# A hybrid diffusion-transformer block on one Trainium2 core: the softmax shift of the grouped-query attention in one step, its bound as the exponentials' bias, and one tile in ten cast by GpSimd

## The reference, cut to what matters

```python
q_l = apply_rope(rms_norm(q_l, qk_g_q[l]), cos, sin)
k_l = apply_rope(rms_norm(k_l, qk_g_k[l]), cos, sin)
k_c = rms_norm(k_c, qk_g_k[l])
gqa_l = gqa_latent(q_l, concatenate([k_c, k_l]), concatenate([v_c, v_l]))

s = jnp.einsum('bqkgd,bskd->bkgqs', qg, k).astype(jnp.float32) * ATTN_SCALE
p = jax.nn.softmax(s, axis=-1).astype(v.dtype)
o = jnp.einsum('bkgqs,bskd->bqkgd', p, v)
```

## Time and profile before

| | us |
|---|---|
| runs | 1312.24, 1308.78, 1311.92 |
| median | 1311.92 |
| the profiled execution | 1312.07 |
| its span, first to last instruction | 1310.3 |
| TensorE busy in it | 1261.5 |
| VectorE busy | 941.1 |
| ScalarE busy | 660.0 |
| GpSimd busy | 295.4 |

### The profile page before, as it was taken

One profiled execution on the slowest core, in us unless ns is written; L12 is line 12 of the kernel. 1 busy time (PEld: TensorE's weight loads), 2 busy tenths in 40 slices (PEclk: granted clock), 3 DMA queues, 4 the chain that ended last, 5 costly groups with the idle time before them and its releaser, 6 DMA issues. The chain is left out here.

```text
span 1310.3 us, 22666 instructions
## 1 busy us (share of the span) xinstructions
PE 1261.5 (96%) x7808; PEld 655.4 (50%) x7808; DVE 941.1 (72%) x1577; ACT 660.0 (50%) x1256; POOL 295.4 (23%) x285
## 2 busy tenths in 40 slices
PE   7999999999898999999999999999999999999997
PEld 1564656444674566665455444444444444444443
DVE  3879887576688999983356976666666666566387
ACT  2532124444697999993225554444445444312225
POOL 0100000121133678851002233333322220000001
PEclk9999999999999999999999999999999999999999
DMA  9637712051330131011112122222322204997953
GB/s 374 231 106 284 285 33 65 1 162 65 103 142 1 34 128 32 0 33 49 49 49 81 50 85 71 77 80 80 88 88 88 80 24 146 312 341 257 361 186 131
DMA packets 106708, 158.89 MB, mean 121 GB/s; under 512 B 8208, under 2 KB 67088, under 8 KB 104848
## 3 DMA queue, kind: packets, MB, share of 16 engines
q1 hardware_dynamic: 106640, 158.00, 35.2%
HBM read 135.95 MB, written 19.93 MB: 119 GB/s over the span
## 5 line engine op out<-in xcount | busy, mean ns | idle before, releaser
L1100 PE MATMUL PS<-arena 128*128 128x512 f16 (+9 forms) x7208 | 1212.6, 328 | 29.4 <-DVE arena L2622 9.2
L1100 PEld LDWEIGHTS PS<-arena 128*128 128x128 f16 (+3 forms) x7208 | 604.0, 102 | 608.7 <-issue 60.4
L2702 DVE SCALAR_TENSOR_TENSOR arena<-arena 128x512 f16<-128x512 f32 x148 | 120.9, 823 | 75.6 <-ACT arena L2004 75.6
L2004 ACT ACTIVATE arena<-arena 128x512 f16<-128x512 f32 x140 | 87.6, 629 | 130.4 <-PE PS L1100 130.4
L2116 ACT ACTIVATE arena<-arena 128x512 f16<-128x512 f32 x77 | 48.2, 629 | 130.3 <-DVE arena L2850 72.7
L2607 DVE TENSOR_REDUCE arena<-PS 128x1 f32<-128x512 f32 (+1 forms) x160 | 103.5, 673 | 2.6 <-PE PS L1100 2.5
L1940 ACT ACTIVATE arena<-PS 128x512 f16<-128x512 f32 x160 | 101.4, 634 | 3.1 <-PE PS L1100 2.5
L1015 POOL TENSOR_TENSOR arena<-arena 128x512 f16<-128x512 f32 x64 | 73.9, 1155 | 55.1 <-ACT arena L1943 55.1
L980 POOL TENSOR_TENSOR arena<-arena 128x2 f32<-128x2 f32 (+1 forms) x18 | 21.1, 1172 | 262.1 <-DVE arena L2461 262.1
L1067 POOL TENSOR_TENSOR arena<-arena 128x512 f32<-128x512 f32 x20 | 26.3, 1319 | 221.6 <-DMA arena<-in_w_ffn_in 182.9
L2865 DVE SCALAR_TENSOR_TENSOR arena<-arena 128x512 f16<-128x512 f32 x77 | 52.1, 686 | 28.2 <-ACT arena L2116 28.2
(11 more groups left out here) (199 smaller groups left out, 1120.9 us busy)
## 6 DMA issues: line engine op xcount, KB each, us to landing
arena<-in_w_ffn_out SPq DMA_DIRECT2D x121, 256.0 KB, 5.5
arena<-in_w_mod SPq DMA_DIRECT2D x24, 1024.0 KB, 7.2
arena<-in_w_ffn_in SPq DMA_DIRECT2D x88, 256.0 KB, 3.0
arena<-in_w_in SPq DMA_DIRECT2D x9, 1024.0 KB, 5.4
left_operands<-arena SPq DMA_DIRECT2D x33, 256.0 KB, 2.2
arena<-left_operands SPq DMA_DIRECT2D x3, 2816.0 KB, 14.0
arena<-lay_bias SPq DMA_DIRECT2D x4, 1536.0 KB, 9.6
arena<-in_x SPq DMA_DIRECT2D x2, 2048.0 KB, 13.1
```

What stands on the lines that cost most here:

```text
L1100: return pe.matmul(out, lhsT, rhs, start=start, stop=stop, skip_group_check=True)
L2004: act.activation(aS[n % RING][:, 0], weight_block(p, b), ACT.Copy, scale=WS).then_inc(blk_hi, 1)
L2702: dve.scalar_tensor_tensor(dst[:, 1], src, WS, dst[:, 0], ALU.mult, ALU.subtract).then_inc(blk_lo, 1)
```

## The change

The shift is now one fp16 row: the negated maximum goes straight, rounded to fp16, from the reduction into `shifts`; the row of `lo` stays zero. The same rounded number shifts all scores of a query, so the softmax isn't changed by the rounding. The bound `shift1` isn't added to it any more; it stands as bias (a column of 128x1 in SBUF) in both exponentials, and its factor grows from 1 to 1.125. `mx` is doubled, for the two key heads. Of tile 4 (`CAST_TILE`) ScalarE takes only the fp32 exponential, and GpSimd casts it to fp16 ahead of its subtraction. `pt_hi` isn't counted in this stage any more.

```diff
-POOL_TILES = (1, 4, 6, 8)
+POOL_TILES, CAST_TILE = (1, 4, 6, 8), 4
...
-        mx, nm, rg = f32(3.0, GROUP, 3), f32(3.0625, GROUP), f32(3.09375, 2, GROUP)
+        mx, rg = f32(3.0, 2, GROUP, 3), f32(3.09375, 2, GROUP)
...
                 pool.wait_ge(s_exp, NNA + n + 1)
                 pt = Pt[n % RING_P]
+                if s.i == CAST_TILE:
+                    if n >= RING_P:
+                        pool.wait_ge(o_mm, NNA + n - RING_P + 1)
+                    own.step(pool.tensor_copy(pt[:, 0], Pf[s.full]))
+                    own.wait()
                 pool.tensor_tensor(pt[:, 1], Pf[s.full], pt[:, 0], ALU.subtract).then_inc(pt_lo2, 1)
...
             def turn_shifts(s):
-                pe.wait_ge(sh_rdy, 3 * s.g + 3)
+                pe.wait_ge(sh_rdy, s.g + 1)
...
                 act.wait_ge(st_mm, s.n + 1)
-                if s.s >= RING_P:
-                    act.wait_ge(o_mm, NNA + s.n - RING_P + 1)
-                act.activation(Pt[s.s % RING_P][:, 0], PS[:, s.bank], ACT.Exp).then_inc(pt_hi, 1)
+                if s.i != CAST_TILE:
+                    if s.s >= RING_P:
+                        act.wait_ge(o_mm, NNA + s.n - RING_P + 1)
+                    act.activation(Pt[s.s % RING_P][:, 0], PS[:, s.bank], ACT.Exp, bias=shift1)
                 if s.by_pool and s.s >= NKT:
                     act.wait_ge(pt_lo2, s.ahead(-NKT).n_low())
-                act.activation(Pf[s.full] if s.by_pool else PS[:, s.bank], PS[:, s.bank], ACT.Exp).then_inc(s_exp, 1)
+                act.activation(Pf[s.full] if s.by_pool else PS[:, s.bank], PS[:, s.bank], ACT.Exp, bias=shift1)\
+                    .then_inc(s_exp, 1)
...
                 dve.wait_ge(s_mm, NNA + c.n + 1)
+                if c.i == 0 and c.s >= 2 * NKT:
+                    dve.wait_ge(sh_rdy, c.g - 1)
...
             def query_shifts(c):
 
-                hi, lo = shifts[:, HD:HD + 3 * (P + 1) + 1:P + 1], shifts[:, HD + GROUP:HD + GROUP + 3 * (P + 1) + 1:P + 1]
                 dve.wait_ge(s_max, NNA + c.n + 1)
-                dve.tensor_reduce(nm, mx, AX, ALU.max, negate=True).then_inc(sh_rdy, 1)
-                dve.wait_ge(sh_rdy, 3 * c.g + 1)
-                dve.wait_ge(q2_hi, 1)
-                if c.s >= NKT:
+                if c.s < NKT:
+                    dve.wait_ge(q2_hi, 1)
+                else:
                     dve.wait_ge(sh_mm, c.g)
-                dve.tensor_tensor(hi, nm, shift1.broadcast_to((P, GROUP)), ALU.add).then_inc(sh_rdy, 1)
-                dve.wait_ge(sh_rdy, 3 * c.g + 2)
-                dve.scalar_tensor_tensor(lo, nm, shift1, hi, ALU.add, ALU.subtract).then_inc(sh_rdy, 1)
+                dve.tensor_reduce(shifts[:, HD:HD + (GROUP - 1) * (P + 1) + 1:P + 1], mx[:, c.kv], AX, ALU.max, negate=True)\
+                    .then_inc(sh_rdy, 1)
...
-            own.step(dve.tensor_scalar(shift1, shift1, -2.0 ** -7, math.log(PSC), ALU.mult, ALU.add))
+            own.step(dve.tensor_scalar(shift1, shift1, -1.125 * 2.0 ** -7, math.log(PSC), ALU.mult, ALU.add))
```

More of the change, by code:

```diff
@@ L539, in build @@
         s_max = sem("score_maximum")
-        sh_rdy = sem("shift_steps")
+        sh_rdy = sem("shift_ready")
         sh_mm = sem("shift_transposed")
@@ L2600, in chunk_maximum @@
                 dve.wait_ge(s_mm, NNA + c.n + 1)
+                if c.i == 0 and c.s >= 2 * NKT:
+                    dve.wait_ge(sh_rdy, c.g - 1)
                 ps = PS[:, CHUNK_BANK[c.s % 2]]
                 if c.i < 2 * GROUP:
-                    out = mx[:, c.i // 2, c.i % 2:c.i % 2 + 1]
+                    out = mx[:, c.kv, c.i // 2, c.i % 2:c.i % 2 + 1]
                 else:
                     h = 2 * (c.i - 2 * GROUP)
-                    out, ps = mx[:, h:h + 2, 2], ps.rearrange("p (h k) -> p h k", h=2)
+                    out, ps = mx[:, c.kv, h:h + 2, 2], ps.rearrange("p (h k) -> p h k", h=2)
                 dve.tensor_reduce(out, ps, AX, ALU.max).then_inc(s_max, 1)
```

## The result

The kernel after takes 1325.2 us (median of 4 runs, 1323.54 to 1326.57), the kernel before 1312.08 (4 runs, 1308.78 to 1313.31): a ratio of 1.0103, with a 95% interval of 1.0082 to 1.0125. It is slower by 13.1 us, where 17.5 were forecast. A second series of the same two gave 1325.27 us and a ratio of 1.0093 (1.0075 to 1.0111). The profiled execution took 1325.33 us, with a span of 1323.5, 13.2 more than before.

The account below looks back on a forecast made before the run. ScalarE was taken to pace the grouped-query stage; its group, 11.07 - 0.475 + 19 x 0.093 = 12.36 us, gave -0.5, +2.3, +14.2 and +1.5, together +17.5 us on 1312.1: 1329.6 us, range 1318 to 1336.

Parts of the forecast that it names:

- The bound of the kernel now: Grouped-query stage: ScalarE alone, gapless, makes a group last 11.07 us; VectorE is full in the four groups before 461 us.
- middle groups: Eleven full groups of the grouped-query stage, each 12.36 us in place of 11.07: +14.2 us.
- the entry: Start of the grouped-query stage: TensorE can start the shifts at about 412.97 in place of 413.44, giving -0.5 us.
- the copy of the outputs: ScalarE's 128-partition read of PSUM in each group, given the 0.47 us left of 11.07 after 10.60.
- The shift in one step: VectorE's three small instructions, 1.32 us, become one reduction of 0.2 us; its group falls to about 9.95; 0.47 us gained at entry.
- The cast: Tile 4: ScalarE saves one exponential, 0.475 us a group, 7.6 us in all; GpSimd's group goes from 9.32 to about 10.0.
- The column: Bound as 128x1 SBUF bias: 0.093 us for each of 19 exponentials a group, bounds nothing and 0.11.
- groups 1 to 3: Three groups to 461.39 us take 37.1 us in place of 34.8: +2.3 us.
- the last group and what is behind: Tile 9 before the last copy of shifts and the whole last group: +0.19 + 1.29 = +1.5 us.
- The free bias: Rival: each exponential's bias column costs 0 in place of 0.093 us; a group of 10.6 us, 1301.9 us in all; chance 0.08.
- GpSimd as the bound: Rival: GpSimd paces the groups, for which it would need 12.4 us a group; about 1331 us; chance 0.01.
- The clock's case: Rival: TensorE, idling 1.8 us or more a group, is sometimes granted its lower clock (1.2 GHz); 1330 to 1338 us; chance 0.05.

Follow-up runs that it names:

- e_row_nocast: e_row with CAST_TILE set to None, so ScalarE takes both exponentials of tile 4 again, leaving the one-step shift alone: 1307.3 us, ratio 0.9964 to the kernel before.
- e_cast_only: The kernel before with only the cast of tile 4 moved to GpSimd: 1306.6 us, ratio 0.9960 to the kernel before.
- e_row: The kernel after with the bound written once into the zero row of shifts, no bias column in either exponential: 1301.8 us, ratio 0.9921 to the kernel before.
- e_imm: The kernel after with the number -2.0 as bias of both exponentials, no column, the bound left out: 1303.0 us, ratio 0.9942 to the kernel before.
- e_nocast: The kernel after with CAST_TILE set to None, both exponentials of tile 4 on ScalarE with their column: 1337.3 us, ratio 1.0190 to the kernel before.

## Why the prediction was right, and where it was off

*The bound of the kernel now.* ScalarE paces the middle groups, VectorE the first four: e_row_nocast shows both (middle groups unchanged, the first four and the entry 2.7 us quicker in its profile). What the prediction passed over is how close VectorE was behind: its own group of 11.07 us was stretched by waits that shrink when the others move, and e_cast_only stopped at 10.8. The 0.47 us that its sum left for the copy of the outputs is 0.43 in the timelines; the rest is rounding of the distances.

*The shift in one step.* Priced at 0.2 us on VectorE and 0.47 us at the entry. Measured: 0.11 from its start to the next, and at the entry 0.23 from its start to TensorE's (411.14 to 411.37), where it was 0.71: 0.48 gained.

*The cast.* Priced at 0.475 us a group gained and nothing lost on GpSimd. In e_row it was that: 11.07 to 10.58. GpSimd's sum of 10.0 us a group came out at 9.93.

*The column.* This is the term that was mis-sized. "Two columns cost 0.19, one about 0.093" was taken for each of 19 exponentials: 1.77 us. What it measured, by the timeline after: 0.57 - 0.48 = 0.09 behind an fp16 exponential (9 a group), 0.57 - 0.47 = 0.10 behind an fp32 one in SBUF (4), but only 0.57 - 0.51 = 0.06 behind an fp32 one in PSUM (6): 9 x 0.09 + 4 x 0.10 + 6 x 0.06 = 1.57. The 0.51 had about 0.04 us of something else in it that the column's time covers; what that is, no run separates. The sum was 12.36 for a group; it is 12.16. The bounds, nothing and 0.11, held each of the three. The 93 ns of the Trainium skill (ScalarE: Activation LUTs, section "What ACT_TABLE_LOAD costs") agree with two of the three kinds; for the third the measured 0.06 decides.

*The sum, piece by piece,* forecast against profile: 11 middle groups +14.2 against +12.0; groups 1 to 3 +2.3 against +1.7; the last group and what is behind +1.5 against +1.4. That agreement is luck: the last group gave +1.2 and the low clock just behind the stage +1.7, and 1.4 us of it came back behind 1200 us, where nothing was edited. Further, the first group and the entry -0.5 against -1.9. In the last of these 1.6 us aren't of the change: the first chunk maximum starts at 404.20 in place of 405.79, ahead of any instruction whose kind or number was changed. The low clock falls at other times in the two profiles: over 136 to 142 us it was granted at 0.72 before and at 1.00 after. The copy of the first shifts starts between 411.1 and 414.1 us in the twelve profiles at hand. So of the 4.3 us by which the forecast was too high, about 2.8 are the column (2.2 in the middle groups, 0.6 in groups 1 to 3), and 1.6 are scatter from ahead of the stage. Together +17.5 against +13.2.

*The rivals.* The free bias had 1301.9 us: e_row and e_imm, which take the column away, ran in 1301.8 and 1303.0, so its sum was right and its condition wrong. GpSimd as the bound shows with a second cast (10.7 us a group), not with one. The clock's case isn't there behind the first group of the stage of the kernel after, in two profiles of it, but is in e_nocast, with groups 0.6 us longer; and its place just behind the stage had not been thought of.

## What to carry to other kernels

Where ScalarE paces a stage, count what each instruction reads, not only how many instructions there are: a bias as a column cost each ACTIVATE 0.06 to 0.10 us here, a number in the instruction nothing. A constant for all elements can often ride along elsewhere: here a matmul already adds a row to the scores, and a second row of it, zero after the change, takes the bound once for the whole kernel. And when two engines look full, taking from one alone may bring little: here either part brought about half of what both did. Take from both, then look at the third.

## What the runs showed of the hardware that was not expected

The distance between exponentials that read one column is 0.57 us whatever they write, while without it the one that writes PSUM is followed 0.51 us later and the one that writes SBUF 0.47: the column's time covers the 0.04 us that writing to PSUM added.

A copy on 64 of 128 partitions drains ScalarE on both sides, as a cast or as an ACTIVATE: 0.72 us ahead of it and 0.60 to 0.62 behind, where a copy of 452 elements on all partitions takes its place in the row in 0.43. In the middle groups of both kinds the copy starts 0.02 to 0.03 us after the end of the exponential before it, and the next exponential as long after the copy's end.

A VectorE instruction of 4 elements a partition took between 0.18 and 1.08 us when it read two operands in SBUF (means of 517 ns and 300 ns in two kernels with the same code), and the reduction with one operand 0.17 before and 0.18 after (means over the stage: 166 and 175 ns). The stretched ones end 0.03 us after an instruction of GpSimd. The Trainium skill, SBUF — State Buffer, section "SBUF: two separate sides", has the rule that fits: a VectorE operation with two SBUF inputs and a GpSimd operation that reads SBUF exclude each other for a whole instruction. The trace agrees: 29 of 32 such VectorE instructions of the kernel before end together with one of GpSimd, and those of group 0, with GpSimd idle, took 0.18 and 0.23 us.
